# Depthwise convolution taps on TensorE: four shifts stacked on the contraction rows, four column groups side by side, and two subtractions moved to GpSimd

## The reference, cut to what matters

```python
def conv_module(h, w_pw1, w_dw, b_dw, ln_g, ln_b, w_pw2):
    u = h @ w_pw1                                # 1024 -> 2048
    a, gate = jnp.split(u, 2, axis=-1)
    u = a * jax.nn.sigmoid(gate)
    u = lax.conv_general_dilated(u, w_dw[:, None, :], window_strides=(1,),
        padding=[(15, 15)], dimension_numbers=('NWC', 'WIO', 'NWC'),
        feature_group_count=D_MODEL) + b_dw      # 31 taps, each channel by itself
    u = jax.nn.silu(layer_norm(u, ln_g, ln_b))
    return u @ w_pw2
```

## Time and profile before

| | |
|---|---|
| median of 3 runs | 2349.9 us (2349.07 to 2354.52) |
| the profiled execution | 2348.4 us |
| its span | 2346.1 us |
| mean granted TensorE clock | 0.974 |
| PE / DVE / ACT / POOL busy | 95% / 60% / 34% / 28% of the span |
| loop of the convolution, first sigmoid to the mean's second matmul | 69.7 us to 322.8 us |

### The profile page before, as it was taken

One profiled execution on the slowest core, in us unless ns is written; L12 is line 12 of the kernel. 1 busy time (PEld: TensorE's weight loads), 2 busy tenths in 40 slices (PEclk: granted clock), 3 DMA queues, 4 the chain that ended last, 5 costly groups with the idle time before them and its releaser, 6 DMA issues.

```text
span 2346.1 us, 30707 instructions
## 1 busy us (share of the span) xinstructions
PE 2223.6 (95%) x11666; PEld 1787.7 (76%) x11666; DVE 1417.1 (60%) x1872; ACT 807.3 (34%) x1145; POOL 667.5 (28%) x377
## 2 busy tenths in 40 slices
PE   6999969899999999998999999999997999899997
PEld 5677748788888888885457888887886888788885
DVE  5789982654444445544563754655418552699997
ACT  3212134211111111333663311111322543677775
POOL 0000014233333333431444344444542234011001
PEclk8999979999999999999999999999999999899999
DMA  9455532432222222220002233333232234599996
GB/s 309 156 160 169 198 124 81 179 138 63 63 63 63 63 63 63 66 72 10 10 1 64 83 98 92 97 98 113 72 90 63 63 76 153 188 394 403 406 405 252
DMA packets 248208, 312.12 MB, mean 133 GB/s; under 512 B 13642, under 2 KB 199595, under 8 KB 235827
## 3 DMA queue, kind: packets, MB, share of 16 engines
q1 hardware_dynamic: 236764, 275.33, 34.8%
q0 software_dynamic: 6688, 25.69, 2.8%
q10 hardware_dynamic: 4663, 9.79, 1.1%
HBM read 286.13 MB, written 24.65 MB: 132 GB/s over the span
## 4 chain that ended last, share of the span: by engine, by line
PE 84%; DVE 10%; ACT 2%; POOL 1%; DMA 1%; issue 1%; DVEq 0%; POOLq 0%; SPq 0%; ACTq 0%
PE acc L609 48%; PE acc L3013 8%; PE pb L3031 4%; PE acc L2524 3%; PE acc L2735 2%; PE pa L2749 2%; PE pb L2470 2%; PE pb L2762 2%; PE acc L661 2%; PE acc L643 2%; PE acc L2588 1%; DVE csum L1748 1%; DVE hid_hi L1813 1%; PE acc L690 1%; PE pa L2410 1%
## 5 line engine op out<-in xcount | busy, mean ns | idle before, releaser
L548 POOL TENSOR_TENSOR wlo<-raw,whi 128x1024 fp32r<-128x1024 f32 x180 | 449.5, 2498 | 907.1 <-ACT whi L537 887.0
L537 ACT ACTIVATE whi<-raw 128x1024 fp32r<-128x1024 f32 x188 | 198.4, 1059 | 890.3 <-PE acc L609 836.1
L609 PE MATMUL acc<-ah,whi 128*128 128x256 f32 (+1 forms) x1256 | 393.7, 362 | 5.0 <-DVE sg L2008 2.6
L609 PE MATMUL acc<-al,whi 128*128 128x256 f32 (+1 forms) x1256 | 389.4, 359 | 0.0
L609 PE MATMUL acc<-ah,wlo 128*128 128x256 f32 (+1 forms) x1256 | 388.9, 358 | 0.0
L609 PEld LDWEIGHTS acc<-ah,whi 128*128 128x128 f32 x1256 | 235.6, 189 | 48.3 <-issue 8.9
L609 PEld LDWEIGHTS acc<-ah,wlo 128*128 128x128 f32 x1256 | 236.7, 188 | 36.8
L609 PEld LDWEIGHTS acc<-al,whi 128*128 128x128 f32 x1256 | 236.7, 188 | 36.1 <-issue 0.5
L1833 DVE SCALAR_TENSOR_TENSOR x<-acc,mod,x 128x512 f32<-128x512 f32 (+1 forms) x174 | 109.7, 658 | 232.2 <-PE acc L609 232.1
L1037 DVE TENSOR_TENSOR expert_lo<-expert_pair,expert_hi 128x1024 fp32r<-128x1024 f32 x192 | 224.5, 1219 | 14.5 <-ACT expert_hi L1032 14.5
L1032 ACT ACTIVATE expert_hi<-expert_pair 128x1024 fp32r<-128x1024 f32 x192 | 201.4, 1059 | 63.4 <-PE acc L3013 40.1
(11 more groups left out here) (501 smaller groups left out, 3684.4 us busy)
## 6 DMA issues: line engine op xcount, KB each, us to landing
raw<-in_w_ff SPq DMA_DIRECT2D x128, 512.0 KB, 4.0
mod_raw<-in_w_mod SPq DMA_DIRECT2D x80, 512.0 KB, 5.8
expert_pair<-in_expert_w_gate SPq DMA_DIRECT2D x32, 1024.0 KB, 8.0
expert_pair<-in_expert_w_up SPq DMA_DIRECT2D x32, 1024.0 KB, 7.7
expert_pair<-in_expert_w_down SPq DMA_DIRECT2D x32, 1024.0 KB, 7.3
raw<-in_w_in SPq DMA_DIRECT2D x30, 512.0 KB, 3.8
raw<-in_conv_w_pw SPq DMA_DIRECT2D x24, 512.0 KB, 8.8
expert_rows_dram<-zero_rows POOLq DMA_DIRECT2D x1, 12288.0 KB, 38.1
```

What stands on the lines that cost most here:

```text
L537: e.eng.activation(whi[e.n["q"] % 2][:, :], raw[r][:, :], ACT.Copy).then_inc(S["hi_ready"], 1)
L548: e.eng.tensor_tensor(wlo[b][:, :], raw[e.n["g"] % RING][:, :], whi[b][:, :].bitcast(F32), ALU.subtract).then_inc(S["lo_ready"], 1)
L609: ins = e.eng.matmul(o, w, m, start=keys.index(key) == n, stop=len(keys) - 1 - keys[::-1].index(key) == n)
```

## The change

The taps that PE takes are now done four at a time, and in another shape.

- `shift_rows_of(i)` is new: ACT issues 16 DMAs to a tile, SBUF to SBUF, each 32 partitions by about 3.2 KB. They put four shifts (`SHIFTS = 4`) of the 32 channels of a group `g` on the 128 rows of `shifted[:, g, :]`. There is one such buffer; the DMAs wait for the conv matmuls of the tile before.
- `tap_rows` takes the place of the diagonals: for a block of four taps 128 x 128 values, made by POOL (`place_taps`), one `tensor_tensor` of 128 x 128 to a block.
- `conv_taps(i)` does, for each block and each of the two column ranges (512 and 271), four matmuls with 128 contraction rows and 32 output partitions, one for each channel group.
- PE takes 12 taps of tiles 0 to 5, 16 of tile 6 and 24 of tile 7 (`TAP_BLOCKS`), DVE the other 19, 15 and 7. PE does `conv_taps(i-1)` in the place of `conv_taps(i)`, `conv_taps(6)` right behind the last product, and `conv_taps(7)` behind the chunks 18 to 21. DVE adds PE's sum at the tap `SUMS_AT[i]`, and gates the next tile at `GATE_AT[i]`.
- The two subtractions `wlo` to a tile move from DVE to POOL for the tiles 2 to 7 (those of slots 4 to 15).
- The taps' rows are loaded in another order at the start: 18 small DMAs instead of 12 on ACT's queue before `silu_c`.

```diff
-PE_TAPS = (0, 6, 6, 6, 6, 6, 6, 9)
+SHIFTS = 4
+TAP_BLOCKS = (3, 3, 3, 3, 3, 3, 4, 6)
+GATE_AT = (16, 10, 10, 10, 10, 10, 10)
+SUMS_AT = (18, 15, 15, 15, 15, 15, 13, 6)
...
-    diag = sb("diag", [P, max(PE_TAPS), P], at=h_at + 16384)
+    tap_rows = [sb(f"tap_rows{b}", [P, max(TAP_BLOCKS[b::2]), P], at=h_at + 16384 + 2048 * b) for b in range(2)]
+    shifted = sb("shifted", [P, 4, PAD + CTX + PAD + LAT + 6], at=e_at)
...
+    def by_vector(i):
+
+        return TAPS - SHIFTS * TAP_BLOCKS[i]
...
+        for b in range(4):
+            rows_of_taps(32 * b, 3, TAP_SPLIT + SHIFTS * b, range(KT))
+        rows_of_taps(88, 1, 11, range(KT))
+        rows_of_taps(120, 1, 7, (KT - 1,))
...
-        def make_diagonals(i):
-
-            act.wait_ge(S["taps_ready"], i + 1)
-            if i >= 2:
-                act.wait_ge(S["conv_summed"], i - 1)
-            for j in range(PE_TAPS[i]):
-                t = TAPS - PE_TAPS[i] + j
-                ins = act.activation(diag[:, j, :], mats[:, M_ID, :], ACT.Copy, scale=taps[i % 2][:, t:t + 1])
-            ins.then_inc(S["diag_ready"], 1)
+        def shift_rows_of(i):
+
+            act.wait_ge(S["glu_done"], i + 1)
+            if i:
+                act.wait_ge(S["conv_summed"], i)
+            width = wide + SHIFTS * (TAP_BLOCKS[i] - 1)
+            for g in range(4):
+                for s in range(SHIFTS):
+                    at = by_vector(i) + s
+                    act.dma_start(shifted[32 * s:32 * s + 32, g, 0:width], upb[i % 2][32 * g:32 * g + 32, at:at + width]
+                                  ).then_inc(S["shifted_in"], 16)
...
                 copy_row(chunks[0], pa[:, 0:512])
                 take_taps(i + 1)
-                make_diagonals(i + 1)
+                shift_rows_of(i)
                 if i:
                     copy_row(chunks[1], pa[:, 0:512])
             else:
+                shift_rows_of(i)
                 for n in chunks:
                     copy_row(n, acc[1][:, 512 * (n % 2):512 * (n % 2) + 512])
...
+        def place_taps(i):
+
+            if i >= 2:
+                pool.wait_ge(S["conv_summed"], i - 1)
+            for j in range(TAP_BLOCKS[i]):
+                ins = pool.tensor_tensor(tap_rows[i % 2][:, j, :].rearrange("p (g c) -> p g c", g=4),
+                                         mod_pick[:, :].unsqueeze(1).to_broadcast([P, 4, 32]),
+                                         stacked_taps(by_vector(i) + SHIFTS * j, i).unsqueeze(2).to_broadcast([P, 4, 32]),
+                                         ALU.mult)
+            ins.then_inc(S["diag_ready"], 1)
...
+        for i in range(1, KT - 1):
+            split_first(e, split_low)
+            split_first(e, split_low)
+            if i < KT - 1:
+                place_taps(i + 1)
+            add_tile(i - 1)
+        add_tile(KT - 2)
         split_first(e, split_low)
...
+            for t in range(2, by_vector(i)):
+                if t == SUMS_AT[i]:
                     dve.wait_ge(S["dve_chain"], e.at("c"))
-                    dve.wait_ge(S["conv_summed"], i)
+                    dve.wait_ge(S["conv_summed"], i + 1)
                     TT(csum[0][:, :], csum[0][:, :], pbk[:, 0:wide], ALU.add).then_inc(S["conv_taken"], 1)
...
-                if t in beside:
-                    beside[t]()
+                if i < KT - 1 and t == GATE_AT[i]:
+                    gated(i + 1)
+                    tile_modulation(i)
...
-            pe.wait_ge(S["glu_done"], i + 1)
-            pe.wait_ge(S["diag_ready"], i)
-            if i >= 2:
-                pe.wait_ge(S["conv_taken"], i - 1)
-            count = PE_TAPS[i]
-            for j in range(count):
-                t = TAPS - count + j
-                for c0, c1 in ((0, 512), (512, wide)):
-                    ins = pe.matmul(pbk[:, c0:c1], diag[:, j, :], upb[i % 2][:, t + c0:t + c1], start=j == 0,
-                                    stop=j == count - 1)
+            pe.wait_ge(S["shifted_in"], 256 * (i + 1))
+            pe.wait_ge(S["diag_ready"], i + 1)
+            if i:
+                pe.wait_ge(S["conv_taken"], i)
+            count = TAP_BLOCKS[i]
+            for c0, c1 in ((0, 512), (512, wide)):
+                for j in range(count):
+                    for g in range(4):
+                        part = slice(32 * g, 32 * g + 32)
+                        ins = pe.matmul(pbk[part, c0:c1], tap_rows[i % 2][:, j, part],
+                                        shifted[:, g, SHIFTS * j + c0:SHIFTS * j + c1], start=j == 0, stop=j == count - 1)
...
             mod_chunk(first, pa[:, 0:512], after_product=i > 1)
-            conv_taps(i)
+            conv_taps(i - 1)
...
-        conv_taps(KT - 1)
+        conv_taps(KT - 2)
         pe.wait_ge(S["acc_free"], e.at("u", 2))
...
+        conv_taps(KT - 1)
         for n in LAST_CHUNKS[-2:]:
             turn_mod(n, late_rows(n, 1))
```

More of the change, by code:

```diff
@@ L493, in tap_sources, with stacked_taps @@
         return ((taps[i % 2][:, 0:TAP_SPLIT], cols[:, C_TAP_A:C_TAP_A + 8 * TAP_SPLIT], column(i)),
-                (taps[i % 2][:, TAP_SPLIT:TAPS], cols[:, C_TAP_B:C_TAP_B + 8 * (TAPS - TAP_SPLIT)], column(i)))
+                (taps[i % 2][:, TAP_SPLIT:TAP_SPLIT + SHIFTS], cols[:, C_MORE_TAPS:C_MORE_TAPS + 8 * SHIFTS], column(i)))
+    def by_vector(i):
+        return TAPS - SHIFTS * TAP_BLOCKS[i]
+    def stacked_taps(first, i):
+        at = {11: C_VEC + 88 + 4 * i, 7: C_VEC + 120}.get(first, 384 + 8 * (first - TAP_SPLIT) + 4 * i)
+        return cols[:, at:at + 4]
     def chunk_at(n):
@@ L1191, in _, with rows_of_taps @@
             row += 8 * count
-        dw = A["conv_w_dw"][0].rearrange("t (c p) -> (t c) p", p=P)
         act.dma_start(vec_rows[0:120, 2, :], dw[0:120, :]).then_inc(S["consts_in"], 16)
-        act.dma_start(vec_rows[0:128, 3, :], dw[120:248, :]).then_inc(S["consts_in"], 16)
+        def rows_of_taps(row, n, first, tiles):
+            count = 4 * len(tiles)
+            act.dma_start(vec_rows[row:row + count, n, :].rearrange("m (s c) -> m s c", s=SHIFTS),
+                          A["conv_w_dw"][0][first:first + SHIFTS, P * tiles[0]:P * tiles[-1] + P].rearrange(
+                              "s (m c) -> m s c", c=32)).then_inc(S["consts_in"], 16)
+        for b in range(4):
+            rows_of_taps(32 * b, 3, TAP_SPLIT + SHIFTS * b, range(KT))
+        rows_of_taps(88, 1, 11, range(KT))
+        rows_of_taps(120, 1, 7, (KT - 1,))
         act.wait_ge(S["cols_ready"], 1)
@@ L1561, in add_tile @@
                                ).then_inc(S["cv_added"], 1)
-        for i in range(KT - 1):
-            add_tile(i)
-        e.n["g"] = e.n["q"] = 2 * KT
+        def place_taps(i):
[7 more added lines that the diff above has]
+            ins.then_inc(S["diag_ready"], 1)
+        pool.wait_ge(S["cols_ready"], 1)
+        pool.wait_ge(S["prepared"], 3)
+        place_taps(0)
+        place_taps(1)
+        e.n["g"] = e.n["q"] = 4
+        for i in range(1, KT - 1):
[5 more added lines that the diff above has]
+        add_tile(KT - 2)
         split_first(e, split_low)
@@ L1669, in _ @@
         dve.wait_ge(S["vec_turned"], 1)
-        for n, rows in enumerate((96, 88, 120, 128)):
+        for n, rows in enumerate((128, 124, 120, 128)):
             ins = dve.tensor_copy(cols[:, P * n:P * n + rows], pbk[:, P * n:P * n + rows])
@@ L1729, in conv_tile @@
                 dve.wait_ge(S["cv_ready"], i)
-            late = 6 if i == KT - 1 else None
-            if PE_TAPS[i] and not late:
-                dve.wait_ge(S["conv_summed"], i)
[L1733 to L1741, removed]
+            TS(csum[1][:, :], here[:, 1:1 + wide], part[:, 1:2], None, ALU.mult)
+            e.step(TS(csum[0][:, :], here[:, 0:wide], part[:, 0:1], part[:, TAPS:TAPS + 1], ALU.mult, ALU.add))
+            for t in range(2, by_vector(i)):
+                if t == SUMS_AT[i]:
                     dve.wait_ge(S["dve_chain"], e.at("c"))
-                    dve.wait_ge(S["conv_summed"], i)
+                    dve.wait_ge(S["conv_summed"], i + 1)
                     TT(csum[0][:, :], csum[0][:, :], pbk[:, 0:wide], ALU.add).then_inc(S["conv_taken"], 1)
-                    dve.wait_ge(S["conv_taken"], i)
+                    dve.wait_ge(S["conv_taken"], i + 1)
                 if t > 3:
@@ L2392, in _ @@
             turn_tokens(b)
-        pe.wait_ge(S["consts_in"], 16 * 12)
-        for n, rows in enumerate((96, 88, 120, 128)):
+        pe.wait_ge(S["consts_in"], 16 * 18)
+        for n, rows in enumerate((128, 124, 120, 128)):
             ins = pe.transpose(pbk[:, P * n:P * n + rows], vec_rows[0:rows, n, :], ident[0:rows, 0:rows])
@@ L2422, in turn_mod @@
             for j in range(4):
-                ins = pe.matmul(at[:, 2 * j:2 * j + 2], mod_row[n % 2][:, P * j:P * j + P], mod_pick[:, :],
+                ins = pe.matmul(at[:, 2 * j:2 * j + 2], mod_row[n % 2][:, P * j:P * j + P], mod_pick[:, 0:2],
                                 start=True, stop=True)
```

22 lines of the change are left out of this document (9 added, 13 removed).

## The result

The changed kernel takes 2396.2 us (2394.9 to 2404.1, 4 runs) and the kernel before 2352.2 us beside it (4 runs): a ratio of 1.019, 95% interval 1.0165 to 1.0222. The prediction said 2357.8 and at most 2373. The sign was right and the size was not.

The account below looks back on a forecast made before the run. PE's list, and a chain of gate, DVE's sums, cv and ACT's list with 1.6 us to spare, bound the kernel. 2348.4 - 3.1 + 16 - 4 - 1 = 2356.3, median 1.5 higher: 2357.8; range 2331 to 2373.

Parts of the forecast that it names:

- PE's taps: PE's tap matmuls in a tile: three blocks take 4.7 us, against 8.17 before, with the four groups side by side.
- POOL's hold-up of DVE: DVE's sums behind the gate wait for POOL's subtractions, so cv comes at +17.3 us, against +17.04 before.
- The price of an issue: ACT's 16 shift issues ahead of the second row's copy: 0.38 us each, 6.1 us a tile.
- Rival 1: ACT's issues are dear: at 0.60 us each, 3.5 us more a tile, 2378 us in all; chance 0.10.
- The clock in the tile: PE behind its 6.6 us idle: 9.4 us from the row's copy to the next sigmoid, no slow clock counted.
- The other terms of ACT's list: ACT behind cv: taps 0.5 us, the row's copy 0.6, and the diagonals' 1.8 gone.
- the 33.9 us of the forecast: A tile from sigmoid to sigmoid, 3.2 us longer than before; five tiles add 16 us.
- Start: Up to tile 2: small DMAs hidden, and PE gains 3.1 us in tile 1, limited by the second chunk's data.
- End: Last sigmoid to the end of the mean's matmul: +38.3 us against 42.2 before, a gain of 4.
- Norm: The norm's stretch: other matmuls there may be faster, a gain between 0 and 4 us, taken as 1.

Follow-up runs that it names:

- e3_dve_low: The changed kernel with its twelve subtractions moved back from POOL to DVE: 2387.6 us, ratio 1.015.
- e4_before_pool: The kernel before with only the two subtractions of a tile moved to POOL: 2349.6 us, ratio 1.0004.
- e9_fill: The changed kernel with 18 unread matmuls on PE in its wait ahead of the second turn, from the third tile on: 2391.6 us, ratio 1.0186.
- e6_narrow: The changed kernel with the 16 shifts of tiles 1 to 5 and 7 moving only a fifth of their bytes: 2394.7 us, ratio 1.0186.
- e5_twice: The changed kernel with each of a tile's 16 shift transfers issued as two, same bytes: 2465.3 us, one run.
- e1_copy_first: The changed kernel with ACT copying the second chunk's row before it issues the 16 shifts: 2337.1 us, ratio 0.993.
- e11_copy_again: The changed kernel with ACT copying the second chunk's row before the shifts, run again with more rounds: 2338.5 us, ratio 0.9955.

## Why the prediction was wrong

By its own steps, against the trace of after:

- **PE's taps**: 4.7 predicted for three blocks, 4.13 measured; 5.47 for four blocks (6.3 predicted) and 8.4 for six (9.4). The four groups run side by side. Right.
- **POOL's hold-up of DVE**: `cv` at +17.3 predicted, at +16.3 measured. Right, and shown by e3_dve_low and e4_before_pool. The 0.46 us for a block of tap rows was near the 0.40 that it takes alone; beside the sums it took 1.1.
- **The price of an issue**: this step failed. I took 0.38 us, between the 0.42 of the 13 at the start and the 0.344 of the 128-row ones. It is 0.64 from one to the next, above both ends that I kept, 0.28 and 0.60. 16 issues took 10.2 us instead of 6.1, 4.1 us a tile, 20 in five. Rival 1 had the mechanism, put its price at 0.60 and gave it a chance of 0.10; the single issue of 0.60 was the nearest to it, and I had averaged it away.
- **The clock in the tile**: this term was missing. The sum had PE idle for 6.6 us in each tile and still gave what follows at the full-speed 9.4 us. It took 12.6. I had used, which show the clock at 0.50 behind an idle stretch of PE, for the end only. e9_fill puts it at 2.5 us a tile; 3.2 is what the tile above shows. 12 to 16 us in five, by the traces.
- The other terms of ACT's list were small: the taps' 0.5 us went beside the first issue. With 4.1 + 3.2 - 1.0 - 0.4 the 33.9 us of the forecast become 39.8, and 39.87 was measured in that tile.
- **Start**: 3.1 us of gain predicted, none came (sigmoid of tile 2 at 130.19, before 129.68). The step had the second chunk of tile 1, chunk 7, landed by 108.3, as in before. The chain of after has
```profile
101.78 9.24 DMA mod_raw<-in_w_mod
```
  for its last piece, which PE got at 111. Why it came later is open. It was not the bytes of tile 1's shifts: in e6_narrow, which moves a fifth of them, PE starts on that piece at 109.97, 40.7 us behind the first sigmoid (69.24), and in after at 111.07, 40.7 behind its own (70.39).
- **End**: +38.3 predicted, +41.35 measured. I had let the shifts share the rate with the weights, and priced it too low. Chunk 21 was through at 356.7, +28.2 and not +21.8. e6_narrow, with a fifth of the shifts' bytes, has its end at +37.3, 4.1 us sooner, so their bytes cost 4. The rest goes, as I read it, with the dear issues, which end at +15.9 and not at +12.4. By luck the error looks smaller than it was: the taps of tile 7 ran at the full clock in 8.4 us where I had counted 9.4 and 2 more.
- **Norm**: 1 us predicted, nothing came: 23.73 us from the mean to the first matmul behind the norm, 23.74 before.

In us, at the norm: issues 20, clock 14, start 3.6, end 3.1, norm 1, less 7 for the earlier `cv` and the hidden taps of five tiles, make 35. Missing were 44.1 - 7.9 = 36.2; the last us is open.

So the path was right (`cv`, ACT's list, the row's copy, PE's second turn), and that the kernel came out slower follows from it. What failed is one price in that sum and one term that it left out.

## What to carry to other kernels

In these runs DMA issues that stand in a compute engine's list cost that engine by their number (0.64 us each), not their bytes, and what matters is what stands behind them: put the copy that another engine waits for ahead of them. Issuing them from another engine was not tried. When a sum gives an engine an idle stretch, price what follows it at the lower clock too. And transfers that nobody waits for can still take rate from those that somebody does, as at the end of this convolution; look at who else is loading in their stretch.

## What the runs showed of the hardware

- An SBUF-to-SBUF issue of 32 rows takes ACT 0.61 us with 3.2 KB rows, with half of that and with a fifth (e5_twice, e6_narrow), against 0.344 for the experts' stores from SBUF, 128 rows each.
- With the full rows of those transfers among the work of the DMA engines, and not a fifth of them, their busy share is the same 1.06 and the rate is 294 GB/s instead of 363 (after and e6_narrow).
- POOL's blocks of 128 x 128 take 0.40 us each alone and also beside a DVE instruction with one operand in SBUF and one in PSUM (L1777 of after at 105.80), and 1.1 beside DVE's sums with both in SBUF.
- The same kernel goes through the same 400 us of matmuls at two paces, with a granted clock of 1.00 in both. e1_copy_first, then e11_copy_again; the count behind the busy time is PE's matmuls:

```profile
536.74:936.74 400.00, 400.00 (x2265) 346.84 (x2265) 185.04 (x191) 50.87 (x48) 126.88 (x48) 1.00 0.20 62
```
```profile
537.54:937.54 400.00, 400.00 (x2313) 352.81 (x2312) 188.73 (x196) 52.49 (x50) 131.03 (x49) 1.00 0.21 64
```
